# A hybrid gMLP/mLSTM block with expert-choice experts: where the final norm loads, scales and keeps its output tiles

## What is computed

```python
def reference(x, ..., w_gate_e, w_up_e, w_down_e, final_g):
    ...
        h2 = rms_norm(x, norm_ffn_g[l]) * (1.0 + sc2) + sh2
        x = x + g2 * expert_choice_ffn(h2, w_router[l], w_gate_e[l], w_up_e[l], w_down_e[l], cap_lat)
    return rms_norm(x, final_g)

def expert_choice_ffn(h, w_router, w_gate, w_up, w_down, capacity):
    aff = jax.nn.softmax(jnp.einsum('bnd,de->bne', h, w_router).astype(jnp.float32), axis=-1)
    gate, idx = lax.top_k(jnp.swapaxes(aff, 1, 2), capacity)
    xe = jax.vmap(lambda hb, ib: hb[ib])(h, idx)
    a = jnp.einsum('becd,edf->becf', xe, w_gate)
    u = jnp.einsum('becd,edf->becf', xe, w_up)
    ye = jnp.einsum('becf,efd->becd', jax.nn.silu(a) * u, w_down) * gate[..., None]
    scatter = lambda ib, yb: jnp.zeros((n_tok, d), yb.dtype).at[ib.reshape(-1)].add(yb.reshape(-1, d))
    return jax.vmap(scatter)(idx, ye)
```

## Time and profile before

| | |
|---|---|
| median of 3 executions | 1755.61 us (1753.72 to 1756.02) |
| profiled execution, its own time | 1758.14 us |
| its span, first to last instruction | 1756.3 us |
| mean granted TensorE clock | 0.973 |
| busy: PE, DVE, ACT, POOL | 94%, 77%, 60%, 8% of the span |
| chain that ended last, by engine | PE 89%, DVE 6%, ACT 2%, DMA 2% |

### The profile page before, as it was taken

How to read it: one execution, slowest core, us unless ns; L and a number is a source line. 1 busy time by engine, 2 the same in 40 slices (tenths; PEclk the granted TensorE clock), 3 DMA queues, 4 the chain that set the end, 5 groups by cost and what they waited for, 6 DMA issues and landing times.

```text
span 1756.3 us, 21846 instructions
## 1 busy us (share of the span) xinstructions
PE 1658.2 (94%) x8208; PEld 1371.3 (78%) x8216; DVE 1350.3 (77%) x1293; ACT 1046.6 (60%) x985; POOL 143.9 (8%) x137
## 2 busy tenths in 40 slices
PE   6999999999999259999999999999999999999995
PEld 2698987879878248888888888888888888888884
DVE  4575544318864679898989889989889899899897
ACT  5252221236631237777777777777777777777775
POOL 3002100002100010100101101101101001011000
PEclk9999999999989569999999999999999999999998
DMA  9115521111232659999999999999999999999996
GB/s 346 63 52 172 175 98 49 48 48 49 86 120 108 227 177 381 373 379 393 371 384 388 370 388 390 370 390 383 370 399 375 383 390 368 389 387 371 392 384 236
DMA packets 204441, 492.81 MB, mean 281 GB/s; under 512 B 5717, under 2 KB 18809, under 8 KB 204393
## 3 DMA queue, kind: packets, MB, share of 16 engines
q1 hardware_dynamic: 187616, 435.30, 66.6%
q0 software_dynamic: 13248, 47.09, 8.8%
q10 hardware_dynamic: 3528, 9.75, 1.4%
HBM read 471.07 MB, written 21.05 MB: 280 GB/s over the span
## 4 chain that ended last, share of the span: by engine, by line
PE 89%; DVE 6%; ACT 2%; DMA 2%; issue 1%; ACTq 0%; DVEq 0%; POOL 0%; POOLq 0%
PE ps L1120 85%; PE ps L1559 2%; PE ps L1510 1%; DVE topi L2084 1%; DVE topv L2083 1%; DVE affT L2086 1%; DMA moda<-in_w_mod 1%; DVE ring L2167 1%; PE ps L1449 0%; ACT hs L938 0%; PE ps L1139 0%; DVE wl L2134 0%; DVE wol L1966 0%; DVE bns L1932 0%; DMA mbw<-in_w_mod 0%
## 5 line engine op out<-in xcount | busy, mean ns | idle before, releaser
L2134 DVE TENSOR_TENSOR wl<-ring,wh 128x2048 fp32r<-128x2048 f32 x384 | 877.4, 2289 | 106.5 <-ACT wh L1064 106.2
L1064 ACT ACTIVATE wh<-ring 128x2048 fp32r<-128x2048 f32 x384 | 737.1, 1920 | 281.9 <-PE ps L1120 281.2
L1120 PE MATMUL ps<-wh,xeh 128*128 128x512 f32 x1024 | 405.3, 396 | 0.6 <-DVE xel L2114 0.6
L1120 PE MATMUL ps<-wh,xel 128*128 128x512 f32 x1024 | 401.8, 392 | 0.0
L1120 PE MATMUL ps<-wl,xeh 128*128 128x512 f32 x1024 | 276.9, 392 | 0.0
L1120 PEld LDWEIGHTS ps<-wh,xel 128*128 128x128 f32 x1024 | 193.1, 189 | 41.4
L1120 PEld LDWEIGHTS ps<-wl,xeh 128*128 128x128 f32 x1024 | 192.8, 188 | 41.7
L1120 PEld LDWEIGHTS ps<-wh,xeh 128*128 128x128 f32 x1024 | 192.8, 188 | 41.2 <-DVE xel L2114 1.0
L1120 PE MATMUL ps<-wh,hidh 128*128 128x512 f32 x512 | 202.9, 396 | 0.0
L1120 PE MATMUL ps<-wh,hidl 128*128 128x512 f32 x512 | 200.1, 391 | 0.0
L1120 PE MATMUL ps<-wl,hidh 128*128 128x512 f32 x512 | 138.3, 392 | 0.0
(11 more groups left out here) (369 smaller groups left out, 2015.6 us busy)
## 6 DMA issues: line engine op xcount, KB each, us to landing
ring<-in_w_gate_e SPq DMA_DIRECT2D x64, 2048.0 KB, 9.1
ring<-in_w_up_e SPq DMA_DIRECT2D x64, 2048.0 KB, 8.6
ring<-in_w_down_e SPq DMA_DIRECT2D x64, 2048.0 KB, 10.4
mbw<-in_w_mod POOLq DMA_DIRECT2D x32, 512.0 KB, 5.3
hpr<-in_w_in SPq DMA_DIRECT2D x12, 1024.0 KB, 5.5
moda<-in_w_mod SPq DMA_DIRECT2D x3, 2048.0 KB, 21.2
xs<-in_x POOLq DMA_DIRECT2D x8, 512.0 KB, 8.4
wor<-in_w_out SPq DMA_DIRECT2D x2, 2048.0 KB, 7.9
```

What stands on the lines that cost most here:

```text
L1064: act.activation(whv[m % 4], eview(m), ACT.Copy).then_inc(hi_done, 1)
L1120: return pe.matmul(o, l, r, start=start, stop=stop)
L2134: dve.tensor_tensor(wlv[m % 4], eview(m), whv[m % 4].bitcast(F32), ALU.subtract).then_inc(lo_done, 1)
```

## The change

Tiles 0 to 4 of the final norm get buffers of their own (`fin`, in the region `TAIL`, which nothing uses any more in the experts), tiles 5 to 7 lie in ring slot 0. GpSimd's queue loads all eight: 0 to 4 right behind its gather of `tok`, 5 to 7 when half pieces 0 to 17 of the last expert are done. Five tiles are rooted and scaled inside the last expert, behind half pieces 16, 18, 20, 22 and 23. Of the other three, VectorE scales tile 5 behind the expert, tile 6 between the sum into `tok` and the sum of squares, tile 7 between that and the last reciprocal; ScalarE roots all three right behind the expert.

```diff
--- before.py
+++ after.py
@@ -83,7 +83,9 @@
     DK = KT * W // D
     DC = DE // P // DK
     EC = 2 * GUC + DC
-    EARLY = 3
+    FT = 5
+    FIN_AT = [16, 18, 20, 22, 23]
+    EARLY = len(FIN_AT)
     assert EC % ESLOT == 0 and MOD_A == 4 and MOD_B == 8 and WAVE == 6
 
     es = ExitStack()
@@ -431,7 +433,7 @@
             return ps[:, a:b, :].rearrange("p b n -> p (b n)")
 
         whv = [wh[:, i, :] for i in range(4)]
-        finv = ring[:, :, :, :].rearrange("p s k n -> p (s k n)").rearrange("p (t d) -> p t d", t=NT)
+        fin = [at(TAIL + t * 4 * KB if t < FT else RA + (t - FT) * 4 * KB, f"fin{t}", [P, D]) for t in range(NT)]
 
         def eview(m):
 
@@ -643,6 +645,10 @@
             pool.indirect_dma_start(
                 out=tok[:, :], out_offset=None, in_=stream,
                 in_offset=bass.IndirectOffsetOnAxis(ap=idx_u[:, NE - 1:NE], axis=0)).then_inc(xe_in, 16)
+            for t in range(NT):
+                if t == FT:
+                    pool.wait_ge(lo_done, 2 * EC * (NE - 1) + 2 * (EC - MSLOT - 1))
+                pool.dma_start(fin[t][:], stream[t * P:(t + 1) * P, :]).then_inc(fin_in[t], 16)
             pool.wait_ge(out_in, 16 * NT)
             pool.wait_ge(tok_ready, 2)
             pool.indirect_dma_start(
@@ -713,13 +719,9 @@
                     sp.wait_ge(lo_done, e * (2 * EC) + 2 * (m - ESLOT + 1))
                     load(e, m)
 
-            sp.wait_ge(lo_done, 2 * EC * (NE - 1) + 2 * (EC - 2))
-            sp.wait_ge(added, 16 * (NE - 1))
-            for t in range(NT):
-                sp.dma_start(finv[:, t, :], stream[t * P:(t + 1) * P, :]).then_inc(fin_in[t], 16)
             for t in range(NT):
                 sp.wait_ge(fin_ready, t + 1)
-                sp.dma_start(out[0][t * P:(t + 1) * P, :], finv[:, t, :]).then_inc(out_in, 16)
+                sp.dma_start(out[0][t * P:(t + 1) * P, :], fin[t][:]).then_inc(out_in, 16)
             sp.wait_ge(out_in, 16 * NT)
 
         @block.scalar
@@ -1067,7 +1069,7 @@
                 act.wait_ge(fin_in[t], 16)
                 if t >= 1:
                     act.wait_ge(froot_ready, t)
-                link(act.activation(xe[:], finv[:, t, :], ACT.Square, accum_out=stat[:, 0, t:t + 1]))
+                link(act.activation(xe[:], fin[t][:], ACT.Square, accum_out=stat[:, 0, t:t + 1]))
                 act.activation(stat[:, 1, t:t + 1], stat[:, 0, t:t + 1], ACT.Sqrt, bias=epsc[:],
                                scale=1.0 / D).then_inc(froot_ready, 1)
 
@@ -1075,8 +1077,8 @@
                 for m in range(2 * EC):
                     if not first or m >= 4:
                         split_high(e, m, first)
-                    if last and m >= 2 * EC - EARLY:
-                        final_root(m - 2 * EC + EARLY)
+                    if last and m in FIN_AT:
+                        final_root(FIN_AT.index(m))
                     if m % 4 == 3 and 7 <= m < 4 * GUC + 4:
                         q = (m - 7) // 4
                         act.wait_ge(mm_done, e * (2 * EC) + 4 * q + 4)
@@ -2156,15 +2158,15 @@
                                           hidh[:, 4 * q:4 * q + 4].bitcast(F32), ALU.subtract).then_inc(hidl_done, 1)
                     if not last_one and m in (21, 23):
                         features_low(e + 1, (m - 21) // 2)
-                    if last_one and m >= 2 * EC - EARLY:
-                        final_scale(m - 2 * EC + EARLY)
+                    if last_one and m in FIN_AT:
+                        final_scale(FIN_AT.index(m))
 
             def final_scale(t):
                 dve.wait_ge(froot_ready, t + 1)
                 link(dve.reciprocal(stat[:, 2, t:t + 1], stat[:, 1, t:t + 1]))
                 if t == 0:
                     dve.wait_ge(gains_in, 32)
-                dve.scalar_tensor_tensor(out=finv[:, t, :], in0=finv[:, t, :], scalar=stat[:, 2, t:t + 1],
+                dve.scalar_tensor_tensor(out=fin[t][:], in0=fin[t][:], scalar=stat[:, 2, t:t + 1],
                                          in1=fgrow[:], op0=ALU.mult, op1=ALU.mult).then_inc(fin_ready, 1)
 
             dve.wait_ge(idx_ready, 1)
@@ -2181,8 +2183,7 @@
             with dve.Fori(2, NE - 1) as e:
                 expert(e, False, False)
             expert(NE - 1, False, True)
-            for t in range(EARLY, NT):
-                final_scale(t)
+            final_scale(EARLY)
 
 
             dve.wait_ge(added, 16 * (NE - 1))
@@ -2196,8 +2197,10 @@
             for n in range(2):
                 dve.tensor_tensor(tok[:, n * W:(n + 1) * W], tok[:, n * W:(n + 1) * W],
                                   yw[:, n * W:(n + 1) * W], ALU.add).then_inc(tok_sum, 1)
+            final_scale(EARLY + 1)
             dve.wait_ge(tok_sq, 2)
             dve.tensor_tensor(lastst[:, 1, 0:1], lastst[:, 0, 0:1], lastst[:, 0, 1:2], ALU.add).then_inc(tok_sq, 1)
+            final_scale(EARLY + 2)
             dve.wait_ge(tok_root, 1)
             link(dve.reciprocal(lastst[:, 2, 1:2], lastst[:, 2, 0:1]))
             for n in range(2):
```

## The result

The changed kernel takes 1759.21 us (median of 15 runs, 1756.85 to 1763.61) against 1754.72 us (15 runs, 1753.69 to 1758.78) for the kernel before on the same chip: a ratio of 1.0026 with a 95% interval of 1.0018 to 1.0034, or +4.5 us. A repeat later gave 1758.83 against 1754.56 us, 1.0029 [1.0018, 1.0040]; one execution of the kernel before, which took 4339 us there, is not in the ratio. The forecast was 1758.8, and +3.2.

What follows compares the result with a forecast made beforehand. VectorE's tile scalings, 4.6 us past TensorE's last matmuls, were taken to bound the end. With TensorE's stop replacing them, +0.8 (weighted output) and +2.4 (tail) gave 1755.61 + 3.2 = 1758.8 us, range 1755.0 to 1763.0.

Steps and rivals of the forecast that it cites:

- The bytes: Last expert's DMA: five early tile loads make the first down piece land 6.4 us late, 19 us after issue.
- The product: Fourth quarter of the hidden rows: late weights and added work ahead of VectorE's product delay TensorE's transposes by 5.0 us.
- Scalings at 20 to 23: Roots and scalings at half pieces 20, 22 and 23, behind the product: cost nothing, with 1.6 us of cover.
- The weighted output: VectorE's last weighted output starts 0.3 us behind TensorE's end, at 1742.5 against 1741.74: +0.8 us.
- The tail: From weighted output to final scatter: scalings 6 and 7 and the wait for the eighth tile write add 2.4 us.
- GpSimd's issues: Issuing the early tile loads takes GpSimd about 0.53 us each while it has nothing else to do: free.
- The sum: Whole kernel: +0.8 at the weighted output and +2.4 in the tail make +3.2 us, 1758.8 us; chance 0.42.
- the clock: Rival: TensorE's clock falls after a stop longer than 2.3 us, +4.9 to +7.8, about 1761.9 us; chance 0.27.
- The table switch: Rival: each ScalarE table switch costs twice its load, 2.6 us, giving +4.4, 1760.0 us; chance 0.03.
- The bytes not in the way: Rival: first down piece 2.6 us late at most, TensorE stops 1.9 us, no change, 1755.7 us; chance 0.20.
- Faster: Rival: early scalings slip into idle time and TensorE does not stop, -2.1 to -4.6 us; chance 0.08.
- the ceiling: End of the last expert: VectorE's tile scalings alone take 4.6 us past TensorE, the most that moving them can return.

Runs made afterwards that it cites:

- Number 2: The changed kernel, but tiles 0 to 4 loaded at the start of the first expert, so the output omits the experts; ratio to the kernel before 0.9998.
- 6: The changed kernel with five roots and scalings behind half pieces 19 to 23 and all tile loads on SP's queue behind the last weight piece; ratio 1.0010.
- 8: As 6, with the tail of the kernel before and tiles 3 to 7 multiplied by the final gain on GpSimd; ratio 1.0048.
- 3: The changed kernel with tiles 6 and 7 scaled behind tile 5, ahead of the weighted output, as in the kernel before; ratio 1.0018.
- 4: The changed kernel with five scalings from half piece 19 on, each root at the end of its iteration; loads unchanged; ratio 1.0006.
- 9: The changed kernel with tiles 0 and 1 loaded early, the rest by SP behind the weights, six scalings inside the expert, only tile 7 behind; ratio 0.9990.
- 10: As 9, but with five scalings inside the last expert, from half piece 19 on; 1753.43 us, ratio 0.9990.

## Why the prediction was right, and where its sizes were off

- **The bytes.** Forecast: the first down piece 6.4 us late, 19 us from issue to landing. Measured: 7.4 us late, 20.05. The DMA rate and the whole of the five tiles ahead of it were right (the fifth, issued in 1686.3 to 1686.8, lands 16.3 us later, before it); why 1 us more than the tiles' own bytes, no run tells. The forecast let the down piece alone set the rest; the up piece before it is late as well (18.8 us to landing), and in the repeat ScalarE lost most of its time there.
- **The product, +5.0 us on TensorE.** Measured +6.0 and, in the repeat, +4.9. Number 2 gives 1.85 us for ScalarE's and VectorE's added work alone. That the repeat agrees with the forecast to 0.1 us is luck: its +4.9 is 2.94 us of stops and 1.6 of the clock, where the forecast had one stop and no fall.
- **Scalings at 20 to 23 at nothing, with 1.6 us of cover.** VectorE's wait ahead of the weighted output is 1.53 us. Right. The late tiles 5 to 7 delayed nothing.
- **The weighted output, +0.8 us.** It starts 67.31 us behind the scatter against 65.73: +1.6, the 0.8 and the product's missing 1.0, less the 0.2 by which it follows TensorE sooner (0.1 us for 0.3).
- **The tail, +2.4 us.** Measured 8.52 - 6.48 = +2.0: the eighth write is issued 5.6 us behind the start of the output as forecast (5.7), it takes 2.63 us, and GpSimd follows after 0.27 where 0.5 was taken.
- **GpSimd's issues, "free".** They were put at nothing, and cost 0.63 us at the end of the span. From the start of the last scatter to the end of the span it is 8.08 us before, 8.09 and 8.07 in numbers 6 and 8, where GpSimd loads no tile, 8.22 and 8.20 with two loads, and 8.70 to 8.78 in the seven profiles in which it loads all eight. The issues themselves lie under idle time, and the last scatter lands 3.3 to 3.4 us after its issue in all twelve, so the end grows behind that landing; by what way, no row shows.
- **The sum**, +3.2, becomes 1.6 + 2.0 + 0.6 = +4.25 in the first profile (+3.20 in the repeat's) and +4.5 and +4.3 in the times; the tail's 0.4 too much hid a part of what was missing. The forecast called +3.2 the likeliest, just inside the 3.5 us that tell it from no change; the measured +4.5 is just outside.

The rivals: *the clock* is half right. It fell in one of the two profiled executions of the change, and in numbers 3, 4 and 8. The mechanism and the point from which it decides were near (stops of 2.29, 2.44, 2.57, 4.21 and 4.68 us were followed by 0.50, those of 1.15, 1.68 and 1.89 us were not), but the 3.71 us of the first execution was not followed by a fall either, so a stop's length alone doesn't decide. Its price in the change was the lower end I had, 1.6 us and not 4.6, and it isn't added to a stop of 5 us: the up piece's lateness splits the stop in two, as the argument against it said. So the time with a fall is about that without one, +3.2 in the repeat, and not the +6.3 of the rival. *The table switch* costs its load and no more: the two roots differ by 2.64 - 1.37 = 1.27 us, the load is 1.28. The Trainium skill (ScalarE: Activation LUTs, "What ACT_TABLE_LOAD costs") adds a drain of 1.38 us, of which neither the roots of before nor these show anything. *The bytes not in the way* fell with the 20.05 us, and number 2 shows that its arithmetic for that case was right. *Faster* would have needed both the bytes and the added tail gone; numbers 9 and 10, which have most of that (two tiles' bytes, a tail of 7.05 us for 6.48), gain 1.8 us at most, not the 4.6 of the ceiling.

## What to carry to other kernels

A load that is moved ahead of others in a full DMA cost nothing here up to the slack of whoever waits for the pieces behind it, and about its whole time beyond that, where what waited was on the path: look for the slack (3.4 us here, two tiles of five), move that much, and put the rest behind the last weight piece. Work that is taken off an engine's end only pays down to what bounds the end next, and where the work goes instead (ahead of a product that another engine waits for, between the last rows) it is on a path again. Where work moves to the end, list all that the final instruction waits for: here a write that nobody had waited for became the last.

## What the runs showed of the hardware that was not expected

- **GpSimd and VectorE slow each other down** in float32 operations with two operands in SBUF: the 128x2048 subtraction took up to 4.46 us instead of 2.29 and the 128x1024 scaling up to 3.23 instead of 1.28, while GpSimd's 128x1024 multiply took 3.6 (number 8). Early in the same execution, where VectorE mostly reads PSUM, GpSimd's multiply of about half the size takes 1.05 us:

```profile
400.83 1.05 POOL L595 TENSOR_TENSOR vw<-vt,cols 128x516 f32<-128x516 f32 x1 [3.63 <-PE ps L1131]
```

  By that, 128x1024 alone would be some 2.1 us (an estimate). VectorE's added time is near this in both operations (2.17 and 1.95 us at most), as if each had stood for one whole instruction of GpSimd's; no run separates that from sharing. The Trainium skill (GPSIMD Engine Reference, "Specifications") names this contention, for VectorE operations with two SBUF inputs, and the unharmed `hidl` with its PSUM input agrees; that section gives no price, and here it was 1.8 to 2.5 times the length.
- **DMAs issued by GpSimd lengthen the end of the program**: 0.6 to 0.7 us where it issued all eight tile loads, 0.1 for two, nothing where SP issued them (12 profiles). In number 2 five of the eight were issued at the first expert, some 1000 us earlier, and the end is as long, so it goes by their number. It grows behind the landing of the last scatter, where no engine is busy; the span is read to 0.1 us, so the 0.1 for two is at the limit of the reading.
- **TensorE's clock behind a stop is not decided by the stop's length alone**: 1.00 throughout behind 3.71 us, 0.50 behind 2.29, 2.44, 2.57, 4.21 and 4.68 us, as behind the 2.31 and 3.62 us of the earlier trace rows. What else decides was not tried.
